# Gated linear attention in one fp32 block kernel: chunk states replaced by direct products, and two output projections in another block order

## The chip, the cores and the metric

One NeuronCore of one Trainium2 chip runs the whole program. The metric is the device time of one execution in microseconds (us), lower is better. The kernel before has a median of 998.92 us over 3 runs (998.89, 998.92, 1001.28).

## The reference

All is float32, 256 tokens, width 1024. Block one is a layer with gated linear attention (GLA) and a layer with sliding-window attention, each with a squared-ReLU MLP; block two has two further attentions, a gated output and an MLP. The change touches the GLA mixer and the code of two projections (`a_w_out` behind the GLA, `w_out_2` in block two). The GLA, cut to what matters:

```python
# 4 heads, key width 128, value width 256, NC = 4 chunks of C = 64 tokens
bcum = jnp.cumsum(heads(gk, GLA_HK), axis=-2)          # log decay inside a chunk
q_t = qf * jnp.exp(bcum);  k_t = kf * jnp.exp(-bcum)
attn = jnp.where(causal, jnp.einsum('nbhik,nbhjk->nbhij', q_t, k_t), 0.0)
o_intra = jnp.einsum('nbhij,nbhjv->nbhiv', attn, vf)
k_dec = kf * jnp.exp(b_last - bcum)
def step(S, xs):
    q_c, k_c, v_c, bl = xs
    o = jnp.einsum('bhik,bhkv->bhiv', q_c, S)
    S = S * jnp.exp(bl)[..., 0, :, None] + jnp.einsum('bhjk,bhjv->bhkv', k_c, v_c)
    return S, o
_, o_inter = lax.scan(step, S0, (q_t, k_dec, vf, b_last))
o = rms(o_intra + o_inter) * g_onorm * silu(gate)
return o @ w_out
```

## The kernel before

The tokens lie in two halves of 128 partitions (c or c2 = 0, 1). Each large weight matrix streams in blocks of 1 MB (2048 columns on 128 partitions). SP loads block j into `raw`; ACT copies it to `whi` as fp32r (`highs_to`), DVE subtracts to get the remainder `wlo` (`lows_to`), and TensorE multiplies activations with both: per k tile two products with `whi` and one with `wlo`. Each of the three buffers has three slots. ACT may fill `whi` for block j once TensorE is through with block j-3; SP may load `raw` for block j once DVE has made the `wlo` of block j-3.

In `gemm_b` a block holds 4 k tiles by 512 columns. TensorE uses it for token half 0 and then for token half 1: 8 products with `whi` and 4 with `wlo`, 512 columns each, for each half. I call these 12 products a block half. A column half f of a 1024-wide result takes two blocks, so four block halves, and all of it is finished before the next column half begins.

The order of work is written out by hand. Each engine has its own program (`tensor_program`, `vector_program`, `scalar_program`, `pool_program`, `sync_program`); Python generators interleave the small attention steps (`attn_gla`, `gates`) between the block halves. Products of the attention run as plain fp32; one such product shows as two records in the trace (a transposition as one). Small products of fp32 write PSUM banks 4 to 7 in turn (`misc`), block results banks 0 to 3 in pairs (`acc_pair`).

The GLA steps on TensorE, between the last blocks of the values `v` and the first of the gates `gt`:

- `kdt`: 8 transpositions of the decayed keys `kd`; ACT copies them out.
- `at`: 8 products of 128 by 128 for the scores inside chunks; DVE copies them under a mask (`copy_predicated`) into `AT`.
- `gs`: 12 products of 256 columns on 64 rows, keys by values, for chunks 0 to 2; DVE copies the first and adds the decayed state before it to the others (`ST`).
- `o`: per token half and pair of heads, 2 products of 256 columns `AT` by `V`, and 64-row-wide results `qt` by `ST` for each chunk but the first; 8 of the first kind and 12 of the second.

ACT copies `o` to `O`, DVE sums squares, POOL makes the factor `o_rstd` by a power, DVE makes the normed and gated `O`. For columns 0 to 511 it folds gate and gain into one factor before the power is there:

```python
t = stt(s, s, st[:, 24 + h * 2 + c:25 + h * 2 + c], g_, ALU.mult, ALU.mult)
if h == 1:
    t.then_inc(*K.up("gated", 0))
```

`turn_parts("to", V.O, half, ...)` on TensorE waits for the event `gated` 0 or 1 and transposes 4 column tiles of `O` (8 transpositions); ACT and DVE split them into `yT`. `gated` 0 is waited for before the last block half of the gates, `gated` 1 inside `project`, behind the first block half of the projection:

```python
g = gemm_b((name,), w, 0, D, xT, lambda k: K.empty((turned, k // 4, (k // 2) % 2)))
next(g)
hook()
```

The blocks of `project` run in the order (k tiles 0-3, columns 0-511), (4-7, 0-511), (0-3, 512-1023), (4-7, 512-1023). DVE adds each finished result to `x`, TensorE transposes the first half of `x` for the next norm before the last block half (`norm_early`).

Of the kernel before, what the change touches and what calls it, by code (L numbers as in the profile page):

```python
# [134 lines left out]
class Views:  # L135


    def __init__(self, S, A):
# [22 lines left out]
        self.kdt = M[:, 7168:8192]  # L161
# [3 lines left out]
        self.ST = M[:, 14336:17408]  # L165
# [68 lines left out]
STEPS = [(p, c) for p in range(2) for c in range(2)]  # L234

# [24 lines left out]
def tensor_program(pe, K, V):  # L260
# [327 lines left out]
    kdt, kt_, qt, VV, AT, ST = V.kdt, V.kt, V.qt, V.V, V.AT, V.ST  # L588
# [52 lines left out]
    def attn_gla():  # L641
        for h2 in range(2):
            tile = ("kdt", h2)
            b = take(tile, misc())
            for w in due(K.at("kd")):
                pe.wait_ge(*w)
            for j in range(2):
                h = 2 * h2 + j
                for c in range(2):
                    t = tr(b[:, j * 256 + c * 128:j * 256 + c * 128 + 128],  # L650
                           V.kd[:, h * 256 + c * 128:h * 256 + c * 128 + 128])
            t.then_inc(*K.filled(tile))
# [12 lines left out]
        v_ready = [K.empty(("v", f, c)) for f in (0, 512) for c in range(2)]  # L665
        def states(h2, *chunks):

            banks_ = [take(("gs", c, h2), misc()) for c in chunks]
            for w in due(K.empty(("kdt", 1)), *v_ready):
                pe.wait_ge(*w)  # L670
            for j in range(2):
                h = 2 * h2 + j
                for c, b in zip(chunks, banks_):
                    rows = slice(64 * (c % 2), 64 * (c % 2) + 64)
                    t = mm(b[:, j * 256:j * 256 + 256],
                           kdt[rows, h * 256 + (c // 2) * 128:h * 256 + (c // 2) * 128 + 128],
                           VV[rows, c // 2, h * 256:h * 256 + 256], True, True)
                    if j == 1:
                        t.then_inc(*K.filled(("gs", c, h2)))

        states(0, 0, 1)
        yield
        states(1, 0, 1)
        yield
        states(0, 2)
        states(1, 2)
        yield
        for c2 in range(2):
            for h2 in range(2):
                tile = ("o", c2, h2)  # L690
                b = take(tile, misc())
                for w in due(K.empty(("at", 1)), K.empty(("gs", 2 * c2, 1))):
                    pe.wait_ge(*w)
                for j in range(2):
                    h = 2 * h2 + j
                    mm(b[:, j * 256:j * 256 + 256], AT[:, h * 256 + c2 * 128:h * 256 + c2 * 128 + 128],
                       VV[:, c2, h * 256:h * 256 + 256], True, False)
                    for c in (2 * c2, 2 * c2 + 1):
                        if c:
                            rows = slice(64 * (c % 2), 64 * (c % 2) + 64)  # L700
                            t = mm(b[rows, j * 256:j * 256 + 256], qt[:, h * 256 + c * 64:h * 256 + c * 64 + 64],
                                   ST[:, (c - 1) * 1024 + h * 256:(c - 1) * 1024 + h * 256 + 256], False, True)
                t.then_inc(*K.filled(tile))
                yield
        yield
        yield
# [7 lines left out]
    def gates_and_scores():  # L714
        yield from gates()
        yield
        for _ in range(4):
# [5 lines left out]
    for _ in range(6):  # L723
        next(gg)
        next(attn, None)
        next(attn, None)
    run_all((attn, 1))
# [380 lines left out]
def vector_program(dve, K, V):  # L1108
# [159 lines left out]
    def project(name, s, hook):  # L1268
        g = gemm_b(D, 8, lambda f, m, c: add_x((name, f, c), f // 512, c))
        next(g)  # L1270
        hook()
        for _ in range(6):
            next(g)
# [81 lines left out]
    bc, e1, qt, kt_, kd, O, ST, AT = V.bc, V.e1, V.qt, V.kt, V.kd, V.O, V.ST, V.AT  # L1355
# [46 lines left out]
    def gates():  # L1402
# [59 lines left out]
    def attn_gla():  # L1462
        for h2 in range(2):
            yield
# [7 lines left out]
            yield  # L1472
        for c in range(3):
            for h2 in range(2):
                tile = ("gs", c, h2)
                for w in due(K.full(tile), *([K.dma("scr1", 1), K.dma("scr2", 2)] if c == 0 else
                                             [K.empty(("gs", c - 1, 0)), K.empty(("gs", c - 1, 1)), K.at("ebl")])):
                    dve.wait_ge(*w)
                for j in range(2):
                    h = 2 * h2 + j  # L1480
                    o = c * 1024 + h * 256
                    b = K.bank(tile)[:, j * 256:j * 256 + 256]
                    if c == 0:
                        t = dve.tensor_copy(ST[:, o:o + 256], b)
                    else:
                        t = stt(ST[:, o:o + 256], ST[:, o - 1024:o - 768], S["ebl"][:, h * 4 + c:h * 4 + c + 1], b,
                                ALU.mult, ALU.add)
                t.then_inc(*K.emptied(tile))
            yield
        for c2 in range(2):  # L1490
            for h2 in range(2):
                for w in due(K.empty(("o", c2, h2))):
                    dve.wait_ge(*w)
                for j in range(2):
                    h = 2 * h2 + j
                    n = h * 2 + c2
                    s = O[:, c2, h * 256:h * 256 + 256]
                    for w in due(*([ev["sq"]] if "sq" in ev else [])):
                        dve.wait_ge(*w)
                    ev["sq"] = step(dve.tensor_tensor_reduce(S["sq"][:, 0:256], s, s, 1.0, 0.0, ALU.mult, ALU.add,  # L1500
                                                             st[:, 8 + n:9 + n]))
                    K.value["o_ssq", 0] = ev["sq"]
                yield
        yield

        for w in due(K.empty(("gt", 0, 0)), K.empty(("gt", 0, 1)), K.dma("bc", 3)):
            dve.wait_ge(*w)
        gain = S["onorm"].rearrange("p (a n) -> p a n", a=1).broadcast_to([128, 2, 256])
        for c in range(2):
            s = V.GT[:, c, 0:512].rearrange("p (a n) -> p a n", a=2)  # L1510
            t = tt(s, s, gain, ALU.mult)
        d = step(t)
        for w in due(K.at("o_rstd"), d):
# [17 lines left out]
    def gates_and_scores():  # L1531
        yield from gates()
        yield
        for _ in range(4):
# [3 lines left out]
    def gated():  # L1538
        for w in due(ev["on"], K.empty(("gt", 512, 0)), K.empty(("gt", 512, 1))):
            dve.wait_ge(*w)  # L1540
        for c in range(2):
            s = O[:, c, 512:1024]
            t = tt(s, s, V.GT[:, c, 512:1024], ALU.mult)
        t.then_inc(*K.up("gated", 1))
# [3 lines left out]
    for _ in range(6):  # L1548
        next(gg)
        next(attn, None)  # L1550
        next(attn, None)
    run_all((attn, 1))
# [4 lines left out]
    gated()  # L1557
# [426 lines left out]
def scalar_program(act, K, V):  # L1984
# [117 lines left out]
    def project(s, hook):  # L2102
        g = gemm_b(D, 8, lambda f, m, c: None)
        next(g)
        hook()
        for _ in range(6):
# [59 lines left out]
    def gates():  # L2166
# [17 lines left out]
        actf(kd, kd, ACT.Exp, scale=-1.0).then_inc(*K.up("g_ekd"))  # L2184
# [20 lines left out]
    def attn_gla():  # L2205
        for h2 in range(2):
            tile = ("kdt", h2)
            for w in due(K.full(tile)):
                act.wait_ge(*w)
            copy(V.kdt[:, h2 * 512:h2 * 512 + 512], K.bank(tile)).then_inc(*K.emptied(tile))  # L2210
            yield
            yield
        for c in range(3):
            yield
        for c2 in range(2):
            for h2 in range(2):
                tile = ("o", c2, h2)
                for w in due(K.full(tile)):
                    act.wait_ge(*w)
                copy(V.O[:, c2, h2 * 512:h2 * 512 + 512], K.bank(tile)).then_inc(*K.emptied(tile))  # L2220
                yield
        yield
        yield
# [7 lines left out]
    def gates_and_scores():  # L2231
        yield from gates()
        yield
        for _ in range(4):
# [5 lines left out]
    for _ in range(6):  # L2240
        next(gg)
        next(attn, None)
        next(attn, None)
    run_all((attn, 1))
# [315 lines left out]
def pool_program(pool, K, V):  # L2560
# [61 lines left out]
    for w in due(K.at("g_eq")):  # L2622
        pool.wait_ge(*w)
    pool.tensor_copy(S["ebl"][:, :], V.qt.rearrange("p (g t) -> p g t", t=64)[:, :, 63:64].rearrange(
        "p g t -> p (g t)")).then_inc(*K.up("ebl"))
    for w in due(K.at("o_ssq")):
# [283 lines left out]
```

## Time and profile before

| what | value |
|---|---|
| median of 3 runs | 998.92 us |
| the profiled execution | 999.79 us |
| its span, first to last instruction | 998.0 us |
| TensorE busy, weight loads busy | 985.3 us (99%), 835.8 us (84%) |
| DVE, ACT, POOL busy | 665.1, 492.0, 36.6 us |
| chain that ended last | TensorE 96%, DVE 2%, ACT 1% |
| mean granted TensorE clock | 0.999 |
| DMA | 177.55 MB, mean 178 GB/s |

The span is what the profile sees of the program; 1.8 us of the execution lie around it. The busy time of TensorE is the union of its products with modelled ends, so it says that the engine is nearly always at work, but not at what rate. The rate is read from the distance between the starts of neighbouring groups in the timeline.

### The profile page before, as it was taken

The page shows a single profiled execution, that of the slowest core. Times are in us where ns is not written, and L with a number is a line of the kernel's source. Part 1 is how long each engine was busy: PE and PEld are TensorE (multiplying, and loading weights), DVE is VectorE, ACT ScalarE, POOL GpSimd, SP SyncE. Part 2 cuts the span into 40 slices and gives each one's busy share as a digit, 9 for nine tenths or more (in the row PEclk, how much of TensorE's full clock was granted, in tenths as well). Part 3 has the DMA queues.
Part 4 walks back from the last instruction along what each step waited for, and adds up shares of the span by engine and source line. Part 5 has one row for each costly group of instructions (what it writes and reads, how often), then busy time and mean ns, then how long its engine had stood idle before and what let it go on. Part 6 is the DMA issues. An engine that isn't in the chain of part 4 may idle for free.

```text
span 998.0 us, 13064 instructions
## 1 busy us (share of the span) xinstructions
PE 985.3 (99%) x5414; PEld 835.8 (84%) x5414; DVE 665.1 (67%) x935; ACT 492.0 (49%) x581; POOL 36.6 (4%) x71
## 2 busy tenths in 40 slices
PE   8999999999999999999999999999999999999997
PEld 8786788888888878888888889888888888888886
DVE  5875766566657976756566658865756675656665
ACT  4453454444446764544444444354554454444454
POOL 2001000000000001000000012000000000000000
PEclk9999999999999999999999999999999999999999
DMA  8652567767653435876675564434165474455551
GB/s 264 191 188 79 178 167 221 214 197 218 212 207 102 127 113 153 245 224 181 191 233 182 199 209 156 157 132 148 56 235 184 148 253 169 169 191 188 190 190 53
DMA packets 113408, 177.55 MB, mean 178 GB/s; under 512 B 4615, under 2 KB 75923, under 8 KB 113348
## 3 DMA queue, kind: packets, MB, share of 16 engines
q1 hardware_dynamic: 113028, 176.37, 55.5%
q8 instruction: 43, 0.70, 0.3%
q10 hardware_dynamic: 320, 0.34, 0.1%
q14 instruction: 17, 0.14, 0.0%
HBM read 174.86 MB, written 1.83 MB: 177 GB/s over the span
## 4 chain that ended last, share of the span: by engine, by line
PE 96%; DVE 2%; ACT 1%; DMA 0%; POOL 0%; issue 0%; ACTq 0%; DVEq 0%; POOLq 0%
PE ps L290 92%; PE ps L294 4%; DVE M L1128 1%; DVE wlo L1120 1%; DMA ident<-in_c_ident 0%; DVE M L1120 0%; POOL st L2573 0%; ACT M L1999 0%; ACT M L1996 0%; DVE cc L1598 0%; DVE RR L1120 0%; POOL st L2570 0%; DVE x L1120 0%; ACT xs L1996 0%; DVE M L1124 0%
## 5 line engine op out<-in xcount | busy, mean ns | idle before, releaser
L290 PE MATMUL ps<-whi,RR 128*128 128x512 f32 (+1 forms) x1556 | 399.7, 389 | 0.0
L1120 DVE TENSOR_TENSOR wlo<-raw,whi 128x1024 fp32r<-128x1024 f32 (+3 forms) x325 | 374.3, 1194 | 20.7 <-ACT whi L1999 20.3
L1999 ACT ACTIVATE whi<-raw 128x2048 fp32r<-128x2048 f32 x161 | 301.2, 1873 | 166.9 <-PE ps L290 148.4
L290 PEld LDWEIGHTS ps<-whi,RR 128*128 128x128 f32 x1556 | 284.0, 188 | 59.4 <-issue 4.5
L290 PE MATMUL ps<-RR,whi 128*128 128x512 f32 (+1 forms) x1264 | 261.1, 351 | 0.0
L290 PEld LDWEIGHTS ps<-RR,whi 128*128 128x128 f32 x1264 | 200.0, 188 | 28.7 <-issue 3.0
L290 PE MATMUL ps<-wlo,RR 128*128 128x512 f32 (+1 forms) x778 | 220.5, 385 | 0.0
L290 PEld LDWEIGHTS ps<-wlo,RR 128*128 128x128 f32 x778 | 144.2, 188 | 29.6
L1120 DVE TENSOR_TENSOR M<-M,ps 128x512 f32<-128x512 f32 (+1 forms) x57 | 38.7, 682 | 172.0 <-ACT M L1999 167.9
L290 PEld LDWEIGHTS ps<-RR,wlo 128*128 128x128 f32 (+1 forms) x1016 | 138.1, 190 | 9.2 <-DVE wlo L1120 0.7
L290 PE MATMUL ps<-RR,wlo 128*128 128x256 f32 (+1 forms) x1016 | 144.5, 282 | 0.0
L1999 ACT ACTIVATE M<-ps 128x512 f32<-128x512 f32 (+2 forms) x90 | 55.2, 615 | 142.8 <-PE ps L290 117.0
L1999 ACT ACTIVATE RR<-M 128x512 fp32r<-128x512 f32 x48 | 30.4, 633 | 71.1 <-DVE M L1128 71.1
L290 PE MATMUL ps<-M 128*64 128x128 f32 (+7 forms) x424 | 55.3, 335 | 0.4 <-DVE M L1120 0.4
L290 PEld LDWEIGHTS ps<-M 128*64 128x64 f32 (+4 forms) x424 | 35.1, 160 | 13.4 <-issue 9.9
L1999 ACT ACTIVATE RR<-ps,G 128x256 fp32r<-128x256 f32 x64 | 25.4, 476 | 32.2 <-PE ps L294 31.8
L2570 POOL TENSOR_SCALAR st<-st 128x2 f32<-128x2 f32 (+2 forms) x11 | 5.1, 460 | 857.2 <-ACT xs L1996 536.6
L1128 DVE SCALAR_TENSOR_TENSOR M<-M 128x512 f32<-128x512 f32 (+1 forms) x49 | 34.4, 703 | 1.7
L1120 DVE TENSOR_TENSOR RR<-M,RR 128x512 fp32r<-128x512 f32 x48 | 32.8, 684 | 0.0
L294 PE MATMUL ps<-ident,M 128*128 128x128 f32 (+1 forms) x196 | 28.0, 276 | 4.1 <-DMA ident<-in_c_ident 1.7
L294 PEld LDWEIGHTS ps<-ident,M 128*128 128x128 f32 (+1 forms) x196 | 22.5, 140 | 11.1 <-issue 6.3
L1128 DVE SCALAR_TENSOR_TENSOR RR<-ps,G,RR 128x256 fp32r<-128x256 f32 x64 | 26.5, 476 | 6.3 <-ACT RR L1999 6.3
(103 smaller groups left out, 379.0 us busy)
## 6 DMA issues: line engine op xcount, KB each, us to landing
raw<-in_w_up SPq DMA_DIRECT2D x32, 1024.0 KB, 6.4
raw<-in_w_down SPq DMA_DIRECT2D x32, 1024.0 KB, 5.6
raw<-in_w_ff SPq DMA_DIRECT2D x32, 1024.0 KB, 5.3
raw<-in_w_in SPq DMA_DIRECT2D x23, 1024.0 KB, 5.1
raw<-in_a_w_in SPq DMA_DIRECT2D x11, 1024.0 KB, 5.5
raw<-in_a_w_out SPq DMA_DIRECT2D x4, 1024.0 KB, 5.1
raw<-in_b_w_q SPq DMA_DIRECT2D x4, 1024.0 KB, 4.9
raw<-in_b_w_out SPq DMA_DIRECT2D x4, 1024.0 KB, 5.1
```

The costliest lines, as they stand in the source:

```text
L290: return pe.matmul(out, lhsT, rhs, start=start, stop=stop, skip_group_check=True)
L294: return pe.transpose(out, in_, ident[0:n, 0:n])
L1120: return dve.tensor_tensor(out, a, b, op)
L1128: return dve.scalar_tensor_tensor(out=out, in0=a, scalar=s, in1=b, op0=op0, op1=op1)
L1999: return act.activation(out, in_, ACT.Copy, **k)
L2570: return pool.tensor_scalar(out, a, s1, s2, op0, op1)
```

## The change

In the GLA the states are gone. Inside a token half, the second chunk's queries meet the first chunk's decayed keys directly (`ac`, 8 products of 64 by 64, copied by ACT into the empty quarter of `AT`). Across the halves, the queries of chunks 2 and 3 meet the keys of chunks 0 and 1 (`ax`, 4 products of 128 by 128, copied by ACT into `AX`); the decays that lie between are multiplied into the keys (`kx`) and queries (`qx`) first. The output then takes 8 products `AT` by `V` and 4 products `AX` by `V`. DVE has new small multiplications for `kx` and `qx` and none for states; POOL copies one part of `qx`; the norm of `O` no longer folds the gate in, and both column halves are gated by a multiplication of their own. The order of `o` is by pair of heads instead of by token half. In `project` (both uses) the blocks run over all columns for k tiles 0-3 first, and the hook comes behind two block halves.

```diff
+HALVES = [(0, 0), (0, 512), (4, 0), (4, 512)]
...
     def project(name, w, s, turned, hook, xT=yT):
-        g = gemm_b((name,), w, 0, D, xT, lambda k: K.empty((turned, k // 4, (k // 2) % 2)))
+        def products():
+            parts = xT if isinstance(xT[0], list) else [k_tiles(part) for part in xT]
+            for k0, f in HALVES:
+                j, hi, lo = block(w[k0 * 128:k0 * 128 + 512, f:f + 512], 4, 512)
+                if k0 == 0:
+                    for c, n in enumerate(acc_pair()):
+                        take((name, f, c), n)
+                for c in range(2):
...
+                    yield
+        g = products()
+        next(g)
         next(g)
         hook()
-        for _ in range(6):
+        for _ in range(5):
             next(g)
         norm_early(s)
         run_all((g, 1))
...
     def attn_gla():
         for h2 in range(2):
-            tile = ("kdt", h2)
...
             tile = ("at", h2)
...
-        states(0, 0, 1)
-        yield
-        states(1, 0, 1)
-        yield
-        states(0, 2)
-        states(1, 2)
+        b = take(("ax",), misc())
+        for w in due(K.at("kx"), K.at("qx_first"), K.at("qx_late")):
+            pe.wait_ge(*w)
+        for h in range(4):
+            t = mm(b[:, h * 128:h * 128 + 128], V.kx[:, h, :, :].rearrange("p c t -> p (c t)"),
+                   V.qx[:, h, :, :].rearrange("p c t -> p (c t)"), True, True)
+        t.then_inc(*K.filled(("ax",)))
+        b = take(("ac",), misc())
+        for h2 in range(2):
+            for c2 in range(2):
+                for j in range(2):
+                    a = (2 * h2 + j) * 256 + c2 * 128
+                    n = (2 * h2 + c2) * 64
+                    t = mm(b[64 * j:64 * j + 64, n:n + 64], V.kd[:, a:a + 64], qt[:, a + 64:a + 128], True, True)
+        t.then_inc(*K.filled(("ac",)))
+        yield
+        for c2, h2 in ((0, 0), (1, 0), (0, 1), (1, 1)):
...
+                t = mm(out, AT[:, h * 256 + c2 * 128:h * 256 + c2 * 128 + 128], VV[:, c2, cols], True, c2 == 0)
+                if c2:
+                    t = mm(out, V.AX[:, h * 128:h * 128 + 128], VV[:, 0, cols], False, True)
...
# vector_program
-        tt(kd, kd, V.kT, ALU.mult).then_inc(*K.up("kd"))
+        d = step(tt(kd4[:, :, 0:3:2, :], kd4[:, :, 0:3:2, :], kT4[:, :, 0:3:2, :], ALU.mult))
+        tt(V.kx[:, :, 1, :], kd4[:, :, 1, :], kT4[:, :, 1, :], ALU.mult)
+        for w in due(d, K.at("qt")):
+            dve.wait_ge(*w)
+        tt(V.kx[:, :, 0, :], kd4[:, :, 0, :], ebl4[:, :, 1:2].broadcast_to([128, 4, 64]), ALU.mult).then_inc(*K.up("kx"))
+        tt(V.qx[:, :, 1, :], qt4[:, :, 3, :], ebl4[:, :, 2:3].broadcast_to([128, 4, 64]), ALU.mult).then_inc(
+            *K.up("qx_late"))
...
-        gain = S["onorm"].rearrange("p (a n) -> p a n", a=1).broadcast_to([128, 2, 256])
-        for c in range(2):
-            s = V.GT[:, c, 0:512].rearrange("p (a n) -> p a n", a=2)
-            t = tt(s, s, gain, ALU.mult)
...
-                g_ = V.GT[:, c, h * 256:h * 256 + 256] if h < 2 else S["onorm"]
-                t = stt(s, s, st[:, 24 + h * 2 + c:25 + h * 2 + c], g_, ALU.mult, ALU.mult)
-            if h == 1:
-                t.then_inc(*K.up("gated", 0))
+                t = stt(s, s, st[:, 24 + h * 2 + c:25 + h * 2 + c], S["onorm"], ALU.mult, ALU.mult)
...
-    run_all((attn, 1))
+    gated(0)
     early()
     turn_parts("to", 0, None)
     next(gg)
     run_all((gg, 1))
-    gated()
+    gated(1)
# scalar_program
+        for w in due(K.full(("ax",))):
+            act.wait_ge(*w)
+        copy(V.AX, K.bank(("ax",))).then_inc(*K.emptied(("ax",)))
+        for j in range(2):
+            t = copy(at5[0:64, :, j, :, 64:128],
+                     K.bank(("ac",))[64 * j:64 * j + 64, 0:256].rearrange("p (a c t) -> p a c t", a=2, c=2))
# pool_program
+    pool.tensor_copy(V.qx[:, :, 0, :], V.qt.rearrange("p (h c t) -> p h c t", h=4, c=4)[:, :, 2, :]).then_inc(
+        *K.up("qx_first"))
```

The order on TensorE from the third block of `v` on. In these rows `ps<-whi,RR` and `ps<-wlo,RR` are the two parts of a block half, `ps<-ident,M` are transpositions, `ps<-M` the attention's own products. Before, up to the first states, and then one of the places where the output is made:

```order
L294 MATMUL ps<-ident,M 128x128 x4
L290 MATMUL ps<-whi,RR 128x512 x8
L290 MATMUL ps<-wlo,RR 128x512 x4
L290 MATMUL ps<-M 128x128 x4
...
L290 MATMUL ps<-M 128x256 x8
...
L290 MATMUL ps<-M 128x256
L290 MATMUL ps<-M 64x256 x2
L290 MATMUL ps<-M 128x256
L290 MATMUL ps<-M 64x256 x2
```

Now:

```order
L293 MATMUL ps<-M 128x128 x8
L293 MATMUL ps<-whi,RR 128x512 x8
L293 MATMUL ps<-wlo,RR 128x512 x4
L293 MATMUL ps<-M 128x128 x4
L293 MATMUL ps<-M 64x64 x8
L293 MATMUL ps<-whi,RR 128x512 x8
L293 MATMUL ps<-wlo,RR 128x512 x4
L293 MATMUL ps<-M 128x256 x6
L293 MATMUL ps<-whi,RR 128x512 x8
L293 MATMUL ps<-wlo,RR 128x512 x4
L293 MATMUL ps<-M 128x256 x6
```

Of the attention four groups are left, with one block half between each two, where seven groups stood; the transpositions and the alternation of 128-row and 64-row results are gone, and six block halves follow before the transpositions of `O`.

The order on DVE, from the gates' first column half (`M<-ps,st,xs`) to the event `gated` 0. Before:

```order
L1128 SCALAR_TENSOR_TENSOR M<-ps,st,xs 128x512
L1500 ISA dg,st<-M 128x256
L1500 ISA st 128x1
L1500 ISA dg,st<-M 128x256
L1500 ISA st 128x1
L1120 TENSOR_TENSOR wlo<-raw,whi 128x1024 x2
L1120 TENSOR_TENSOR M<-M,bcs 128x512 x2
L1128 SCALAR_TENSOR_TENSOR M<-M,st 128x256 x4
L1128 SCALAR_TENSOR_TENSOR M<-M,st,bcs 128x256 x4
```

Now:

```order
L1123 TENSOR_TENSOR wlo<-raw,whi 128x1024 x2
L1131 SCALAR_TENSOR_TENSOR M<-ps,st,xs 128x512 x2
L1131 SCALAR_TENSOR_TENSOR M<-M,st,bcs 128x256 x8
L1123 TENSOR_TENSOR wlo<-raw,whi 128x1024 x2
L1123 TENSOR_TENSOR M<-M 128x512 x2
```

`gated` 0 was raised by the fourth of the multiplications with `st`; it is now raised by the last row shown, behind all eight and behind the remainder of one weight block, which had stood ahead of them.

The order on TensorE inside the projection, from its first block half. Before:

```order
L290 MATMUL ps<-whi,RR 128x512 x8
L290 MATMUL ps<-wlo,RR 128x512 x4
L294 MATMUL ps<-ident,M 128x128 x8
L290 MATMUL ps<-whi,RR 128x512 x8
L290 MATMUL ps<-wlo,RR 128x512 x4
```

Now:

```order
L293 MATMUL ps<-whi,RR 128x512 x8
L293 MATMUL ps<-wlo,RR 128x512 x4
L293 MATMUL ps<-whi,RR 128x512 x8
L293 MATMUL ps<-wlo,RR 128x512 x4
L297 MATMUL ps<-ident,M 128x128 x8
```

The 8 transpositions that wait for `gated` 1 stand one block half later, counted from the projection's first product.

## Rows read from the trace of the kernel before

**Rows 1.** The page, busy time and share, and the granted clock by slice.

```profile
PE 985.3 (99%) x5414; PEld 835.8 (84%) x5414; DVE 665.1 (67%) x935; ACT 492.0 (49%) x581; POOL 36.6 (4%) x71
...
PEclk9999999999999999999999999999999999999999
```

**Rows 2.** What TensorE waited for between 60 and 200 us: total, times, longest.

```profile
PE ps L294 <- DVE M L1120: 1.1, 1, 1.1
```

**Rows 3.** Timeline of TensorE: start us, busy us, line, tile, records.

```profile
57.41 1.98 PE L290 MATMUL ps<-whi,RR 128*128 128x512 f32 x8
...
60.14 0.60 PE L294 MATMUL ps<-ident,M 128*128 128x128 f32 x4
...
63.35 1.05 PE L290 MATMUL ps<-M 128*128 128x128 f32 x8
64.16 2.07 PE L290 MATMUL ps<-whi,RR 128*128 128x512 f32 x8
...
71.15 2.00 PE L290 MATMUL ps<-M 64*128 64x256 f32 x16
...
83.25 4.80 PE L290 MATMUL ps<-M 128*128 128x256 f32 x20
...
90.83 2.39 PE L290 MATMUL ps<-M 128*128 128x256 f32 x12
...
96.02 1.98 PE L290 MATMUL ps<-whi,RR 128*128 128x512 f32 x8
```

**Rows 4.** Timeline of the weight loads inside `o`, 83 to 88 us.

```profile
84.35 0.30 PEld L290 LDWEIGHTS ps<-M 128*128 128x128 f32 x2 [0.39 <-issue]
84.97 0.19 PEld L290 LDWEIGHTS ps<-M 128*64 128x64 f32 x2 [0.33 <-issue]
85.55 0.30 PEld L290 LDWEIGHTS ps<-M 128*128 128x128 f32 x2 [0.39 <-issue]
```

**Rows 5.** Timeline of TensorE in block two's attention, 690 to 718 us.

```profile
690.84 1.53 PE L290 MATMUL ps<-M 128*64 128x128 f32 x24
692.30 1.13 PE L290 MATMUL ps<-M,xs 128*128 128x256 f32 x4
...
716.17 1.03 PE L290 MATMUL ps<-M,xs 128*128 128x256 f32 x4
717.03 1.03 PE L290 MATMUL ps<-M 128*128 128x256 f32 x4
```

**Rows 6.** Timeline of TensorE in the first projection.

```profile
106.94 1.08 PE L290 MATMUL ps<-wlo,RR 128*128 128x512 f32 x4
109.16 1.07 PE L294 MATMUL ps<-ident,M 128*128 128x128 f32 x8 [1.14 <-DVE M L1120]
109.98 2.10 PE L290 MATMUL ps<-whi,RR 128*128 128x512 f32 x8
```

**Rows 7.** Timeline of DVE, 54 to 109 us, pieces.

```profile
54.01 3.48 DVE L1120 TENSOR_TENSOR M<-M 128x1024 f32<-128x1024 f32 x3
...
91.75 0.75 DVE L1128 SCALAR_TENSOR_TENSOR M<-ps,st,xs 128x512 f32<-128x512 f32 x1 [2.12 <-ACT xs L1996]
...
98.63 1.67 DVE L1128 SCALAR_TENSOR_TENSOR M<-M,st 128x256 f32<-128x256 f32 x4 [0.35 <-POOL st L2573]
...
101.81 2.35 DVE L1120 TENSOR_TENSOR wlo<-raw,whi 128x1024 fp32r<-128x1024 f32 x2
...
107.72 1.29 DVE L1120 TENSOR_TENSOR M<-M 128x512 f32<-128x512 f32 x2
```

**Rows 8.** Timeline of ACT around the output of the attention.

```profile
80.50 0.60 ACT L1999 ACTIVATE M<-ps 128x512 f32<-128x512 f32 x1 [10.35 <-PE ps L290]
...
91.03 0.69 ACT L1996 ACTIVATE xs<-ps,st 128x512 f32<-128x512 f32 x1 [2.34 <-PE ps L290]
```

**Rows 9.** Timeline of POOL, the power for the norm of `O`.

```profile
96.07 2.52 POOL L2573 TENSOR_TENSOR st<-st,half_ 128x8 f32<-128x8 f32 x1
```

**Rows 10.** The page, DMA issues: KB each, us from issue to landing.

```profile
raw<-in_a_w_out SPq DMA_DIRECT2D x4, 1024.0 KB, 5.1
```

More of the change, by code:

```diff
@@ L663, in attn_gla @@
             t.then_inc(*K.filled(tile))
-            yield
[L665 to L669, printed above, removed]
+        yield
[14 more added lines that the diff above has]
+        t.then_inc(*K.filled(("ac",)))
+        yield
+        for c2, h2 in ((0, 0), (1, 0), (0, 1), (1, 1)):
+            tile = ("o", c2, h2)
+            b = take(tile, misc())
+            for w in due(K.empty(("at", 1)), K.empty(("ax",)), K.empty(("ac",)),
+                         *[K.empty(("v", 512 * h2, c)) for c in range(2)]):
                 pe.wait_ge(*w)
@@ L672, in states @@
                 h = 2 * h2 + j
[L673 to L679, printed above, removed]
-        states(0, 0, 1)
-        yield
-        states(1, 0, 1)
-        yield
-        states(0, 2)
-        states(1, 2)
[L687 to L703, printed above, removed]
+                out, cols = b[:, j * 256:j * 256 + 256], slice(h * 256, h * 256 + 256)
+                t = mm(out, AT[:, h * 256 + c2 * 128:h * 256 + c2 * 128 + 128], VV[:, c2, cols], True, c2 == 0)
+                if c2:
+                    t = mm(out, V.AX[:, h * 128:h * 128 + 128], VV[:, 0, cols], False, True)
+            t.then_inc(*K.filled(tile))
+            if c2:
                 yield
-        yield
-        yield
     attn = attn_gla()
@@ L716, in gates_and_scores @@
         yield
-        for _ in range(4):
+        for _ in range(3):
             next(attn)
@@ L1268, in project, with products @@
     def project(name, s, hook):
-        g = gemm_b(D, 8, lambda f, m, c: add_x((name, f, c), f // 512, c))
+        def products():
+            for k0, f in HALVES:
+                take()
+                for c in range(2):
+                    if k0:
+                        add_x((name, f, c), f // 512, c)
+                    yield
+        g = products()
+        next(g)
         next(g)
         hook()
-        for _ in range(6):
+        for _ in range(5):
             next(g)
@@ L1490, in attn_gla @@
[L1490 to L1502, printed above, removed]
+        yield
@@ L1533, in gates_and_scores, with gated @@
         yield
-        for _ in range(4):
+        for _ in range(3):
             next(attn)
             yield
-    def gated():
-        for w in due(ev["on"], K.empty(("gt", 512, 0)), K.empty(("gt", 512, 1))):
+    def gated(half):
+        f = 512 * half
+        for w in due(ev["on"], K.empty(("gt", f, 0)), K.empty(("gt", f, 1))):
             dve.wait_ge(*w)
         for c in range(2):
-            s = O[:, c, 512:1024]
-            t = tt(s, s, V.GT[:, c, 512:1024], ALU.mult)
-        t.then_inc(*K.up("gated", 1))
+            s = O[:, c, f:f + 512]
+            t = tt(s, s, V.GT[:, c, f:f + 512], ALU.mult)
+        t.then_inc(*K.up("gated", half))
     run_all((k_and_v(), 1), (gates_and_scores(), 1))
@@ L2102, in project, with products @@
     def project(s, hook):
-        g = gemm_b(D, 8, lambda f, m, c: None)
+        def products():
+            for _ in HALVES:
+                take()
+                for c in range(2):
+                    yield
+        g = products()
+        next(g)
         next(g)
         hook()
-        for _ in range(6):
+        for _ in range(5):
             next(g)
@@ L2205, in attn_gla @@
     def attn_gla():
-        for h2 in range(2):
-            tile = ("kdt", h2)
+        yield
+        for w in due(K.full(("ax",))):
+            act.wait_ge(*w)
+        copy(V.AX, K.bank(("ax",))).then_inc(*K.emptied(("ax",)))
+        at5 = V.AT.rearrange("p (a j c t) -> p a j c t", a=2, j=2, c=2)
+        for w in due(K.full(("ac",)), K.empty(("at", 1))):
+            act.wait_ge(*w)
+        for j in range(2):
+            t = copy(at5[0:64, :, j, :, 64:128],
+                     K.bank(("ac",))[64 * j:64 * j + 64, 0:256].rearrange("p (a c t) -> p a c t", a=2, c=2))
+        t.then_inc(*K.emptied(("ac",)))
+        yield
+        for c2, h2 in ((0, 0), (1, 0), (0, 1), (1, 1)):
+            tile = ("o", c2, h2)
             for w in due(K.full(tile)):
                 act.wait_ge(*w)
[L2210 to L2220, printed above, removed]
+            copy(V.O[:, c2, h2 * 512:h2 * 512 + 512], K.bank(tile)).then_inc(*K.emptied(tile))
+            if c2:
                 yield
-        yield
-        yield
     attn = attn_gla()
@@ L2233, in gates_and_scores @@
         yield
-        for _ in range(4):
+        for _ in range(3):
             next(attn)
```

76 lines of the change are left out of this document (35 added, 41 removed).

## Prediction

> **What bounds the kernel now.** I read the page first: TensorE is busy 99% of the span and the next engine, DVE, 67% [rows 1]; the granted clock reads 9 (full, the 2.4 GHz level) in every slice. The view of waits has one entry between 60 and 200 us, 1.1 us, on DVE [rows 2]. So what counts is time on TensorE, and waits that the change makes or removes there. Busy time has modelled ends, therefore I price work by the distance between starts in the timeline of TensorE.
>
> The unit is the block half of 12 products: from 57.41 to 60.14 there is one, 2.7 us (2.72 over several) [rows 3]. From the first attention transpositions at 60.14 to the block half at 96.02 there are 35.9 us. By the order of the program 7 block halves lie in it, 7 x 2.72 = 19.0 us. **The attention thus costs TensorE 16.8 us now**, any wait inside included. Those are `kdt`, `at`, `gs` and `o`.
>
> **What the attention costs after the change.** Each kind from its nearest row.
> - `at`, 8 products of 128 by 128, unchanged: four take 64.16 - 63.35 = 0.81 us, and the block half behind them shows 2.07 where it shows 1.98 otherwise [rows 3], so 0.1 at the end of each group: 2 x 0.81 + 0.1 = 1.7.
> - `ax`, 4 products of the same form: 0.8.
> - `ac`, 8 products with 64 columns on both sides, alternating between the two column halves of the array. Nearest are 12 products of 128 columns that alternate in the same way, 692.30 - 690.84 = 1.46 us or 0.24 per pair [rows 5]. Four pairs cost 1.0 if fewer columns save nothing, 0.5 if they halve it. A change between full-width and half-width results has a price as well (next point), 0.2 to 0.4 for the way in and out. I take 0.9 with ends 0.5 and 1.4.
> - `o`, 12 products of 256 columns, all full width. There are two prices. Inside the old `o` a full-width product takes 84.97 - 84.35 = 0.62 us and the half-width one behind it 0.58 [rows 4]. In block two's attention, where no half-width product stands between, two take 717.03 - 716.17 = 0.86, so 0.43 each [rows 5]. The new `o` is in the second situation: 12 x 0.43 + 2 x 0.1 = 5.4 us. With 0.62 it would be 7.6.
>
> The sum is 1.7 + 0.8 + 0.9 + 5.4 + 0.1 behind `ac` = 8.9 us, and **the saving 16.8 - 8.9 = 7.9 us**, between 8.5 (all low ends) and 5.2 (the high `ac` and 0.62 per product).
>
> The Trainium skill, TensorEngine Tiling (Array Packing), Overview, "Key Properties", says that changing the tiling mode drains the engine. By it the 0.62 belongs to the alternation and the new `o` costs 5.4, as the two rows have it. The same page's "Instruction Overhead" speaks against the change, at `ac`: it warns against taking the tiling factor from a dimension that is already small, and puts some 60 cycles of overhead on each product. As an estimate from that page, 16 records at 60 cycles of 2.4 GHz are 0.4 us more, so 1.3 for `ac` and a saving of 7.5; no row here has a product this narrow.
>
> **The waits.**
> - *`gated` 1 (in the projection), removed.* The last part of the block half starts at 106.94 and lasts 0.91 to the next start; the transpositions could start at 107.85 and start at 109.16 [rows 6]: 1.3 us, of which the profile shows 1.14 as idle. Behind two block halves instead of one there are 2.7 us more. The saving is 1.3.
> - *`gated` 0 (before the gates' last block half), new.* I count from E, the end of the gates' fourth block half, the one that completes columns 0 to 511. Now it lies at 90.83 [rows 3]. ACT starts the sigmoid at 91.03 [rows 8], DVE the product with it at 91.75 [rows 7]: E + 0.9. That takes 0.7. Then come, by the new order, 8 multiplications (98.63 to 101.81, 3.2 us), the remainder of a weight block (2.35), and the two gating products (107.72, TensorE starts at 109.16, so 1.4 to the release) [rows 6, 7]. Sum: E + 8.6. TensorE has three block halves and is there at E + 8.2. Before, there was a fourth half and part of the attention behind E, and `gated` 0 waited neither for the last four multiplications nor for the remainder. **A new wait of 0.4 us.**
> - *The remainder itself* is ready at E + 7.2, and TensorE wants it for the third of those halves after its 8 products with `whi`, E + 5.4 + 1.8 = 7.2. That is no margin; but what is lost here is not lost again at `gated` 0, since both hang on one chain.
> - *`gated` 1, second look.* The gates' last half ends near E + 12.2; sigmoid, product and gating take 0.9 + 0.7 + 1.4, so E + 15.2. TensorE arrives two block halves after 12.2, at E + 17.6. No wait, 2.4 us spare.
> - *New work on DVE before the scores.* The three multiplications from 54.01 last 3.5 us [rows 7]; the third becomes four smaller ones with 1280 columns instead of 1024, under 1 us more. `ax` stands 4.5 us behind 60.14, so they end long before. POOL's copy of 256 columns is free in the same way: POOL is busy 4% [rows 1].
> - *New copies on ACT.* `AX` is a copy of 512 columns, 0.6 us, like one that ACT now does after 10.35 us idle [rows 8]; the two for `ac` are smaller. Between `ac` and the first `o` lies a block half of 2.7 us. Cost 0; without that half, some 1.5 us.
> - *POOL's power* takes 2.5 us [rows 9]. The squares are done a few us after the last `o`, three block halves before E, so it ends before E. Cost 0.
> - *Fewer operations on DVE* (12 for the states, 2 for the folded gain, against 2 more gating products) shorten nothing by themselves, as DVE isn't the bound.
> - *The order of the blocks in both projections.* The same products and loads, so 0. Columns 0 to 511 are finished at the sixth block half instead of the fourth; their addition to `x` (0.7 us, as other 512-column operations on DVE) is needed by the transpositions behind the seventh, 2.7 us later. In block two's projection TensorE waits for nothing now, and gains nothing.
>
> **Sum.** 7.9 + 1.3 - 0.4 = 8.8 us. The profiled execution took 999.79 us, so its like should take 991.0; the median shown is 0.9 lower, and against it I get 998.92 - 8.8 = **990.1 us**.
>
> **Rivals.**
> 1. *The chain to `gated` 0 is longer than counted.* The saving on TensorE is there, but it arrives earlier at a chain that runs over ACT and DVE, and each us of slip on it is a us of wait. For it: no margin at the remainder, a table load on ACT, ACT and DVE in written order. Against: DVE has less to do before E. One to 3.5 us of slip: 991.1 to 993.6. Chance 0.13.
> 2. *The full-width products keep their 0.62 us.* For it: it is the row of exactly this product [rows 4]. Against: 0.43 in [rows 5]. 12 x 0.19 = 2.3 us more: 992.4. Chance 0.06.
> 3. *The weights come too late* once TensorE uses them faster. A block takes 5.1 us to land [rows 10], TensorE uses one in 5.4 us elsewhere, and SP may issue it only when a remainder three blocks back is made. If this took back 6 us or more, the result would be within 0.3%: 996 to 998. Against: the rest of the kernel lives at that rate without waits [rows 2]. Chance 0.04.
> 4. *Slower: the clock.* If the wait at `gated` 0 grew to several us, TensorE could drop to its 1.2 GHz level and all that follows would cost twice as much until it rises. To be slower than 998.92 + 3, wait and slow work together must take 11.8 us; a wait of 4 us and 7.8 us of work at half rate would do: 1002. Idle of 1.14 us leaves the clock at full [rows 1, 2], so it decides only from a wait well beyond that. Chance 0.03. The Trainium skill, TensorE: Matmul & The Clock Gate, Part 1, has the half rate as the default that activity releases; by it a long enough idle brings this case about, and no row in this stretch shows it.
>
> **How the numbers follow.** The forecast has 0.74. Its own range is 989.0 to 991.5: ends of the product prices but for rival 2 (0.6 each way), the new wait between 0 and 1 us. The low end of the whole range is 988.8, with a little for the scatter of medians. Upwards it takes in rivals 1 and 2: 993.8. A difference of 0.3%, 3 us, is about what a measurement of this kernel can tell from none. Faster by more than that: 0.74 + 0.13 + 0.06 = 0.93; within it 0.04; slower 0.03.
>
> **What would show it.** In the timeline of TensorE after the change: about 8.9 us of attention beside its block halves, from the first `at` to the end of the last `o`; 0.43 us between starts of the new `o` products (rival 2: 0.62); `ac` in about 0.9 us; a wait for DVE under 1 us before the first transpositions of `O`, none before the second; granted clock 9 throughout. The prediction is wrong if TensorE waits over 1 us anywhere between 60 and 130 us, or if the mlp behind the projection waits for weights.

## Result and profile after

| | before | after |
|---|---|---|
| median | 999.45 us (4 runs, 998.89 to 1001.28) | 990.51 us (4 runs, 990.32 to 991.03) |
| ratio | 1 | 0.9906, 95% interval 0.9895 to 0.9918 |
| span of the profiled execution | 998.0 us | 988.5 us |
| from the first attention group to the end | 937.9 us | 928.2 us |
| waits of TensorE shown between 60 and 130 us | 1.1 us | none |

The forecast was 990.1 us, with 989.0 to 991.5 for its own case. The medians differ by 8.9 us and the ratio says 9.4 (8.2 to 10.5). The fourth row of the table is the one that I compare in all runs: the span less the start of the first attention group on TensorE (60.14 before [rows 3], 60.31 after). What TensorE does ahead of that start, the first blocks, the change doesn't touch; the start itself lies between 59.0 and 61.0 us in the profiled runs, and such a difference would hide terms of a few tenths.

The page of the changed kernel, the lines that answer to [rows 1]:

```profile
PE 977.5 (99%) x5390; PEld 834.8 (84%) x5390; DVE 661.0 (67%) x926; ACT 492.1 (50%) x582; POOL 37.9 (4%) x72
...
PEclk9999999999999999999999999999999999999999
```

TensorE has 7.8 us less busy time, and is still at 99%. DVE has lost 4 us and ACT nothing, and neither would have shown that the kernel became 9 us faster.

The timeline of TensorE after the change (start us, busy us, line, tile, records), to be held against [rows 3] and [rows 6]:

```profile
60.31 1.95 PE L293 MATMUL ps<-M 128*128 128x128 f32 x16
62.01 2.07 PE L293 MATMUL ps<-whi,RR 128*128 128x512 f32 x8
63.92 1.07 PE L293 MATMUL ps<-wlo,RR 128*128 128x512 f32 x4
64.83 1.67 PE L293 MATMUL ps<-M 128*128 128x128 f32 x24
66.42 2.12 PE L293 MATMUL ps<-whi,RR 128*128 128x512 f32 x8
68.38 1.08 PE L293 MATMUL ps<-wlo,RR 128*128 128x512 f32 x4
69.30 2.75 PE L293 MATMUL ps<-M 128*128 128x256 f32 x12
71.70 2.20 PE L293 MATMUL ps<-whi,RR 128*128 128x512 f32 x8
...
74.66 2.75 PE L293 MATMUL ps<-M 128*128 128x256 f32 x12
...
80.02 1.98 PE L293 MATMUL ps<-whi,RR 128*128 128x512 f32 x8
...
92.71 1.10 PE L293 MATMUL ps<-wlo,RR 128*128 128x512 f32 x4
93.92 1.06 PE L297 MATMUL ps<-ident,M 128*128 128x128 f32 x8
...
97.57 1.98 PE L293 MATMUL ps<-whi,RR 128*128 128x512 f32 x8
...
102.10 1.07 PE L293 MATMUL ps<-wlo,RR 128*128 128x512 f32 x4
103.02 1.03 PE L297 MATMUL ps<-ident,M 128*128 128x128 f32 x8
```

From 60.31 to the block half at 80.02 there are 19.7 us with 4 block halves in them, 10.9 us; the attention takes 8.8 us. `at` takes 62.01 - 60.31 = 1.70, `ax` and `ac` together 66.42 - 64.83 = 1.59, six `o` products 71.70 - 69.30 = 2.40. These 2.40 us are not six whole products: the first record of the block half starts 0.03 us behind the last record of the group, and the block half then takes 2.96 instead of 2.72. The price is read inside the group, where a stretch near its end begins with this record:

```profile
71.45 0.59 PE L293 MATMUL ps<-M 128*128 128x256 f32 x2
```

It is the eleventh of the twelve, so ten records take 71.45 - 69.30 = 2.15, and a product of two records 0.43 us. The transpositions at 93.92 start 0.3 us later than the block half ahead of them allows (92.71 + 0.91 = 93.62): that is the new wait at `gated` 0. It is too short for the view of waits; it is found from the starts. Those at 103.02 follow without a gap (102.10 + 0.91).

The granted clock with the stages of both kernels, busy time of TensorE in each (stretch, length, busy, records, clock, DMA share, GB/s). Before:

```profile
60.14:105.08 44.94, 44.94 (x217) 1.00 0.33 117
105.08:130.07 24.99, 23.85 (x113) 1.00 0.73 198
130.07:308.31 178.24, 178.24 (x913) 1.00 0.66 203
```

After:

```profile
60.31:97.57 37.26, 37.16 (x193) 1.00 0.44 143
97.57:121.15 23.58, 23.58 (x113) 1.00 0.72 210
121.15:299.39 178.24, 178.24 (x913) 1.00 0.67 202
```

These are the same stages: attention with the gates, the first projection, the first MLP. They give 7.7, 1.4 and 0.0 us. The three parts sum to 9.1 us, and 0.6 us are missing to the 9.7 us between 937.9 and 928.2: they come behind 299 us, far from the GLA and not in the projection of block two either. No step of the prediction has them. The run banks_back below looks for them.

### The profile page after: what moved, and what is told of

Its sections match the earlier page's. It is cut to its first block, busy times and chain, and to the rows that moved or that the text cites. A ratio compares the mean times of both kernels' runs of the same rounds, so it can differ in the third digit from the quotient of the medians.

```text
span 988.5 us, 13010 instructions
## 1 busy us (share of the span) xinstructions
PE 977.5 (99%) x5390; PEld 834.8 (84%) x5390; DVE 661.0 (67%) x926; ACT 492.1 (50%) x582; POOL 37.9 (4%) x72
## 4 chain that ended last, share of the span: by engine, by line
PE 96%; DVE 2%; ACT 1%; DMA 0%; issue 0%; POOL 0%; ACTq 0%; POOLq 0%
PE ps L293 93%; PE ps L297 4%; DVE wlo L1123 1%; DMA ident<-in_c_ident 0%; DVE RR L1131 0%; DVE M L1131 0%; ACT M L1990 0%; DVE M L1123 0%; ACT M L1993 0%; POOL st L2575 0%; DVE cc L1592 0%; ACT RR L1993 0%; ACT xs L1990 0%; DVE x L1131 0%; DVE x L1123 0%
## 5 line engine op out<-in xcount | busy, mean ns | idle before, releaser
L1993 ACT ACTIVATE M<-ps 128x512 f32<-128x512 f32 (+3 forms) x91 | 55.3, 609 | 128.9 <-PE ps L293 105.6
L293 PE MATMUL ps<-M 128*64 128x128 f32 (+7 forms) x408 | 48.7, 322 | 0.5 <-DVE M L1123 0.5
L1990 ACT ACTIVATE M<-M,cc 128x128 f32<-128x128 f32 (+2 forms) x40 | 21.6, 542 | 17.9 <-DVE cc L1744 9.9
```

Of the source, the lines that this page charges most:

```text
L293: return pe.matmul(out, lhsT, rhs, start=start, stop=stop, skip_group_check=True)
L1990: return act.activation(out, in_, f, **k)
L1993: return act.activation(out, in_, ACT.Copy, **k)
```

## Experiments

All times in the column are the span less the start of the first attention group, from one profiled execution each; the ratio is of the timed runs to those of the kernel before beside them.

| run | start to end, us | against | ratio, 95% interval |
|---|---|---|---|
| before | 937.9 | | |
| after | 928.2 | -9.7 | 0.9906 (0.9895 to 0.9918) |
| gla_only | 929.0 | +0.8 to after | 0.9914 (0.9901 to 0.9928) |
| order_only | 936.5 | -1.4 to before | 0.9983 (0.9974 to 0.9993) |
| gate_early | 927.9 | -0.3 to after | 0.9904 (0.9891 to 0.9918) |
| hook_late_old_order | 930.9 | +2.7 to after | 0.9937 (0.9923 to 0.9950) |
| grouped | 936.4 | -1.5 to before | 0.9985 (0.9975 to 0.9994) |
| ax_ac_mixed | 929.2 | +1.0 to after | a single run |
| ac_twice | 928.7 | +0.5 to after | a single run |
| banks_back | 928.8 | +0.6 to after | a single run |
| gate_later | 929.3 | +1.1 to after | 0.9912 (0.9897 to 0.9927) |
| after_again | 928.2 | 0.0 to after | 0.9898 (0.9884 to 0.9913) |
| gate_early_again | 927.9 | -0.3 to after | 0.9896 (0.9880 to 0.9913) |

The intervals are 0.2 to 0.3% wide, 2 to 3 us. For most of these terms the timed runs only say that nothing large is missing; the terms themselves are read in the timeline.

### The two parts alone

The new GLA with the old `project`:

```diff
+        g = gemm_b((name,), w, 0, D, xT, lambda k: K.empty((turned, k // 4, (k // 2) % 2)))
         next(g)
         hook()
-        for _ in range(5):
+        for _ in range(6):
```

> The new GLA with the old projection code. Theory (TensorE's time is the sum of its work and its waits): gating for gated 1 starts on DVE at 99.57 in the changed kernel and releases 1.4 us later, 101.0; with the old order TensorE gets there at 97.57 + 2.72 = 100.3, so a wait of 0.7 us. Span 988.5 + 0.7 = 989.2 us. Rival (the new projection order gives the whole 1.3 us that it was credited with): span 989.8. Rival (the order does nothing once the GLA is short, since DVE has less to do): 988.5.

TensorE in this run, inside the projection:

```profile
96.52 1.98 PE L293 MATMUL ps<-whi,RR 128*128 128x512 f32 x8
98.33 1.07 PE L293 MATMUL ps<-wlo,RR 128*128 128x512 f32 x4
99.95 1.06 PE L297 MATMUL ps<-ident,M 128*128 128x128 f32 x8 [0.56 <-DVE M L1101]
```

98.33 + 0.91 is 99.24, the transpositions start at 99.95: a wait of 0.7 us, as expected. The span of this run is 988.2 us, which taken by itself would say that nothing was lost; but its first attention group starts at 59.24 instead of 60.31. From there to the end it is 0.8 us longer than the changed kernel. So beside the new GLA, the new order is worth 0.7 to 0.8 us and not the 1.3 us that it was credited with: with the new GLA the chain on DVE is already ahead. The sigmoid of the last gates waits on ACT for a product on DVE; it starts 1.0 us behind the end of the gates in the kernel before (106.11 against 105.08) and 0.4 us behind it here (96.94 against 96.52). The sum of the prediction is right nevertheless, because it counts a wait as removed, by whichever part.

The old GLA with the new `project`:

```diff
+        def products():
+            for k0, f in HALVES:
```

> The old GLA with the new projection code. Theory: TensorE gets to the transpositions for gated 1 one block half later, at 110.6 where the release is at 109.2, so the wait of 1.3 us goes and nothing else changes: span 998.0 - 1.3 = 996.7 us, no wait behind it up to the mlp. Rival (the later finish of columns 0 to 511 moves a wait to norm_early or to the mlp): span 997.3 or more, with a wait of DVE or ACT before the x transpositions.

```profile
109.82 1.08 PE L292 MATMUL ps<-wlo,RR 128*128 128x512 f32 x4
110.73 1.04 PE L296 MATMUL ps<-ident,M 128*128 128x128 f32 x8
111.53 2.09 PE L292 MATMUL ps<-whi,RR 128*128 128x512 f32 x8
```

The wait of [rows 6] is gone and none stands in its place: 1.4 us less from the attention to the end (1.3 expected), span 996.8 us.

Whether it is the order of blocks or the place of the hook was told apart by the old order with the hook behind two block halves:

```diff
         g = gemm_b((name,), w, 0, D, xT, lambda k: K.empty((turned, k // 4, (k // 2) % 2)))
         next(g)
+        next(g)
         hook()
-        for _ in range(6):
+        for _ in range(5):
```

> The changed kernel with the old order of blocks in the projections, the hook still behind two block halves. Theory: the second block now needs k tiles 4-7 at once; the first remainder of the split is on DVE at 104.28 + 0.7 = 105.0 where TensorE is ready at 103.8, so a wait of 1.1 to 1.2 us, and one like it in block two's projection: span 988.5 + 2.3 = 990.8 us. Rival (the place of the hook alone brings the gain, the order of blocks none): 988.5.

```profile
102.95 1.03 PE L297 MATMUL ps<-ident,M 128*128 128x128 f32 x8
105.06 2.09 PE L293 MATMUL ps<-whi,RR 128*128 128x512 f32 x8 [1.07 <-DVE RR L1102]
...
757.77 1.03 PE L297 MATMUL ps<-ident,M 128*128 128x128 f32 x8
759.87 2.08 PE L293 MATMUL ps<-whi,RR 128*128 128x512 f32 x8 [1.07 <-DVE RR L1102]
```

In both projections the block half behind the transpositions starts 2.1 us after them instead of 0.8: 1.3 us each, 2.7 in all (2.3 expected; in each the block half starts 0.1 to 0.2 us later than I had counted). TensorE waits for the split of the tiles that it has just transposed. The late hook needs the new order, since only then do two block halves that don't need them come next.

### The chain to `gated` 0

In the first of these runs DVE norms and gates columns 0 to 511 before the weight remainder and the other columns:

```diff
-        for h in range(4):
-            for c in range(2):
...
-        ev["on"] = step(t)
-        yield
+        for half in range(2):
+            for h in (2 * half, 2 * half + 1):
+                for c in range(2):
...
+            ev["on"] = step(t)
+            if half == 0:
+                gated(0)
+            yield
...
-    gated(0)
     early()
```

> The changed kernel, where DVE norms and gates columns 0 to 511 first (4 multiplications and 2 gating products), then makes the weight remainder, then norms the other columns. Theory: the wait of 0.3 us at gated 0 goes, since its release falls from E + 8.5 to about E + 4.7, and the remainder is ready at E + 6.7 for a need at E + 7.2: span 988.5 - 0.3 = 988.2 us. Rival (the wait is on something else, the transpositions' bank or the sigmoid on ACT): it stays, 988.5.

TensorE and DVE in this run:

```profile
93.42 1.07 PE L293 MATMUL ps<-wlo,RR 128*128 128x512 f32 x4
94.33 1.03 PE L297 MATMUL ps<-ident,M 128*128 128x128 f32 x8
```

```profile
87.76 1.67 DVE L1131 SCALAR_TENSOR_TENSOR M<-M,st,bcs 128x256 f32<-128x256 f32 x4
89.46 1.29 DVE L1123 TENSOR_TENSOR M<-M 128x512 f32<-128x512 f32 x2
90.67 2.35 DVE L1123 TENSOR_TENSOR wlo<-raw,whi 128x1024 fp32r<-128x1024 f32 x2
92.94 1.67 DVE L1131 SCALAR_TENSOR_TENSOR M<-M,st,bcs 128x256 f32<-128x256 f32 x4
```

The gating ends near 90.7 and TensorE comes at 94.33, without a gap (93.42 + 0.91). The time from the attention to the end is 0.3 us less.

In the second run one multiplication more stands ahead of the gating:

```diff
+    tt(e1, e1, bc, ALU.mult)
     gated(0)
     early()
```

> The changed kernel with one more multiplication of 1024 columns on DVE (1.2 us, into a buffer that is not read any more) right before the two gating products of gated 0. Theory (one chain sets the release, and TensorE waits for its end, us for us): the wait before the first transpositions of O grows from 0.3 to 1.5 us, and the time from the first attention products to the end from 928.2 to 929.4 us; the clock stays at its full level. Rival (other work takes the slip up): under 0.6 us more. Rival (the clock falls with the longer wait): over 3 us more.

```profile
93.19 1.12 PE L293 MATMUL ps<-wlo,RR 128*128 128x512 f32 x4
95.54 1.06 PE L297 MATMUL ps<-ident,M 128*128 128x128 f32 x8 [1.23 <-DVE M L1123]
```

The third block half starts at 91.38 and ends at 94.10; the wait is 1.4 us, and the whole is 1.1 us longer. So the chain is one, and rival 1 of the prediction had the right price: the wait grows by 1.1 us for the 1.14 us that DVE is longer at work. The granted clock between 60 and 130 us is 1.00 in this run; an idle of 1.23 us doesn't lower it. Waits of several us, on which rival 4 rested, were not tried.

To see whether gate_early is better in time as well, it ran once more beside the changed kernel:

> The changed kernel as it is, on the chip of the run beside it, to compare with gate_early_again: ratio to before 0.991.

> The changed kernel with columns 0 to 511 normed and gated first, once more, beside the changed kernel itself. Theory: no wait before the first transpositions of O, 0.3 us less than the changed kernel from the first attention products to the end (927.9 against 928.2); in the whole time 0.3 us less, which is less than the scatter of the runs. Rival: no difference in the profile.

The profile repeats itself: 928.2 and 927.9 us, and TensorE's transpositions follow the block half without the gap. The medians are 989.86 and 990.17 us, with runs from 989.13 to 991.57: the 0.3 us can't be told in the time. The profile shows a wait less, and the timed runs show no difference between the two.

### What a product costs beside another width

The kernel before, with each output tile's full-width products first and the half-width ones behind them:

```diff
                     mm(b[:, j * 256:j * 256 + 256], AT[:, h * 256 + c2 * 128:h * 256 + c2 * 128 + 128],
                        VV[:, c2, h * 256:h * 256 + 256], True, False)
+                for j in range(2):
+                    h = 2 * h2 + j
                     for c in (2 * c2, 2 * c2 + 1):
```

This order changes the sums: the second start in a bank comes before the first sum in it is complete, and the outputs are not those of the reference. The number of products and their shapes are the same, so it serves for the time alone. The Trainium skill, PSUM — Partial Sum Buffer, "The four PSUM rules", has a product with the start flag clear the accumulation bits of a whole zero region; by that part of the first sum would be lost, and no run here examined it.

> The kernel before, where each output tile takes its two full-width products first and its half-width ones behind them, so that each of the four tiles changes width 2 times instead of 4. Theory (a change between full-width and half-width results costs 0.19 us each, which is where 0.62 against 0.43 came from): 8 changes less, 1.5 us less; from the first attention transpositions to the end 937.9 - 1.5 = 936.4 us. Rival (0.62 and 0.58 are the price of these products, whatever stands beside them): 937.9.

TensorE, the group that answers to the x20 in [rows 3] and the one behind it:

```profile
82.98 4.11 PE L290 MATMUL ps<-M 128*128 128x256 f32 x20
87.02 2.12 PE L290 MATMUL ps<-whi,RR 128*128 128x512 f32 x8
...
89.89 2.04 PE L290 MATMUL ps<-M 128*128 128x256 f32 x12
91.86 2.11 PE L290 MATMUL ps<-whi,RR 128*128 128x512 f32 x8
```

The x20 group takes 4.04 us instead of 4.73, the x12 group 1.97 instead of 2.32, the tile ahead of them 0.34 us less as well. That is 1.4 us for 8 changes of width, 0.17 each (0.19 expected), and 1.4 to 1.5 us in the whole, the spans being rounded to 0.1. The products are the same in number and shape, so 0.62 was not the price of the product. It closes the sum too: of the 0.62 + 0.58 us in [rows 4] two changes are 0.34, and 0.86 are left for two products, 0.43 for the full-width and 0.43 for the half-width one.

The reverse in the changed kernel, each `ax` product followed by two of `ac`:

```diff
         for h in range(4):
             t = mm(b[:, h * 128:h * 128 + 128], V.kx[:, h, :, :].rearrange("p c t -> p (c t)"),
                    V.qx[:, h, :, :].rearrange("p c t -> p (c t)"), True, True)
+            h2, c2 = h // 2, h % 2
+            for j in range(2):
```

> The changed kernel, where each ax product is followed by two ac products, so 8 changes of width instead of 2 in that group. Theory as in the run before: 6 x 0.19 = 1.1 us more in that group, which takes 1.59 us now: 2.7. Rival (the price lies in the products): 1.6.

```profile
64.75 2.70 PE L293 MATMUL ps<-M 128*128 128x128 f32 x24
67.37 2.11 PE L293 MATMUL ps<-whi,RR 128*128 128x512 f32 x8
```

2.62 us instead of 1.59 for the same 12 products: 1.03 us for 6 changes more, 0.17 each again. The same figure comes from the other side and in another kernel, there with 128 and 64 columns instead of 256: what costs is the change of width, not the product. The 0.17 us are the mean of a way in and a way out. The Trainium skill, TensorEngine Tiling (Array Packing), Overview, "Key Properties", says that a change of mode drains the engine; the traces agree that a change costs time, 0.17 us here; what the engine does in it they don't show.

What is left of the group was measured by doubling `ac`:

```diff
-        for h2 in range(2):
+        for h2 in (0, 1, 0, 1):
```

> The changed kernel with the 8 ac products issued twice over the same outputs. Theory (the group takes 1.59 us, 0.81 of it ax, 0.38 two changes of width, so 0.4 is left for 8 products): 0.4 us more, 2.0 for the group. Rival (a narrow product costs as much as one of 128 columns, 0.24 per pair, and a change of width nothing): 1.0 us more, 2.6.

```profile
63.56 2.13 PE L293 MATMUL ps<-M 128*128 128x128 f32 x40
65.62 2.12 PE L293 MATMUL ps<-whi,RR 128*128 128x512 f32 x8
```

2.06 us against 1.59: 8 narrow products cost 0.47 us, 0.12 per pair. The 0.24 per pair with 128 columns that the prediction took from [rows 5] is too high for a comparison, since those 1.46 us hold a part of the changes of width at both ends. Inside that group of the kernel before, two stretches begin with these records:

```profile
691.22 1.15 PE L290 MATMUL ps<-M 128*64 128x128 f32 x18
...
691.87 0.50 PE L290 MATMUL ps<-M 128*64 128x128 f32 x6
```

Twelve records, three pairs, lie between them: 0.65 us, 0.22 per pair. So half the columns cost a little more than half the time, and what doesn't go with the columns is at most 0.02 us per pair. With two changes of width `ac` is 0.47 + 2 x 0.17 = 0.8 us, and with `ax` 0.8 the group is complete. The estimate of 1.3 us that I made from the same page's "Instruction Overhead", by adding 60 cycles for each record, is too high here. The same passage also has a matmul with a free dimension of 1 take as long as one with 60; by that 64 columns lie just above the limit, and no product here is narrow enough to show it.

### The half microsecond behind 300 us

The GLA used 14 small PSUM tiles before and 8 now, and these take banks 4 to 7 in turn. So each later tile that takes its bank in this turn has another one, two further; some tiles have banks of their own, the query product among them. The profile before has a wait of 0.69 us on ACT at 318.90, ahead of `ps<-dg,ones`, which spreads the norm's factor; after the change there is none. The run turns the banks back:

```diff
+    turn["misc"] += 2
     next(gg)
```

> The changed kernel with the turn of PSUM banks 4 to 7 moved on by two behind the GLA, so that all later small products get the banks that they had before the change. Theory: the product that spreads the norm's factor over the rows, at 309.4 now, takes bank 6 again and waits for ACT's copy of the query product out of it; the wait of 0.7 us on ACT that the kernel before shows at 318.9 comes back, and about 0.5 us in all. Rival (that wait moved with ACT's timing): no wait on ACT there, nothing added.

TensorE there, before:

```profile
317.57 0.64 PE L290 MATMUL ps<-RR,wlo 128*128 128x256 f32 x4
318.90 0.70 PE L290 MATMUL ps<-dg,ones 128*128 128x256 f32 x2 [0.69 <-ACT M L1999]
```

After:

```profile
308.65 0.64 PE L293 MATMUL ps<-RR,wlo 128*128 128x256 f32 x4
309.39 0.70 PE L293 MATMUL ps<-dg,ones 128*128 128x256 f32 x2
```

In banks_back:

```profile
308.87 0.64 PE L293 MATMUL ps<-RR,wlo 128*128 128x256 f32 x4
310.20 0.70 PE L293 MATMUL ps<-dg,ones 128*128 128x256 f32 x2 [0.69 <-ACT M L1994]
```

The wait is back with the same 0.69 us, and the time from the attention to the end rises by 0.6 us, which is all that was missing. In the kernel before this product takes bank 6, out of which ACT must first copy the query product; after the change it takes bank 4, and the query product is in bank 6 as before. The 0.6 us are a by-product of the number of small tiles that the GLA uses.

## Why the prediction was right, and where it was off

- *What bounds the kernel.* Right: every us that TensorE was given or spared is found again in the time from the attention to the end, in all eleven runs.
- *The attention costs 16.8 us now and 8.9 us after.* 8.8 us measured. By kind, expected and measured with the tail behind each group: `at` 1.7 and 1.7 (1.8 with the tail), `ax` 0.8, `ac` 0.9 and 0.1 behind them against 1.59 for both (1.75 with the tail), `o` 5.4 against 2 x (2.40 + 0.24) = 5.3.
- *The choice between 0.62 and 0.43 us per `o` product*, the step with most in it (2.3 us). It was made by what stands beside the product in the row, and is right: 0.43 us inside the group. The two runs on the width show why. Rival 2 falls.
- *`gated` 1, 1.3 us.* The first projection's stage is 1.4 us shorter. The share of the new order in it is 0.7 to 0.8 us beside the new GLA.
- *The new wait of 0.4 us at `gated` 0.* 0.3 us measured. Counted from E, here 85.46, the release was expected at 8.6 and TensorE started at 93.92, E + 8.5. The weight remainder was in time within a few hundredths: the `wlo` part at 92.71 lasts 1.10 instead of 1.07. Rival 1 had the right mechanism, and no slip.
- *Costs set to nothing.* The copies on ACT, POOL's copy and power, the multiplications on DVE and the later sums in `x` added no wait. Rival 3, late weights, falls for the stretch up to the first MLP: that takes 178.24 us in both kernels.
- *What the sum missed.* 0.6 us behind 300 us. No step of the prediction has the turn of the PSUM banks: where it takes the removed tiles out of the attention, it counts the products and copies that go with them, and not that tiles behind them then land in other banks. It adds to the 0.1 us from the attention, 0.1 from the projection and 0.1 from the smaller wait, so that the profile gained 9.7 us where I had 8.8.
- *Luck in the time.* That the median came within 0.4 us of the forecast is in part chance. The forecast starts from a median of 998.92 us before; with the fourth run it is 999.45, 0.5 higher, and this about makes up for the 0.6 us that no step has. The single terms are borne out by the timeline, not by this agreement.
- *Rival 4, the clock.* Not met; the clock is at its 2.4 GHz level in each stretch, with idle up to 1.23 us in gate_later.

## What to carry to other kernels

On an engine that is busy all the time, price work by the distance between starts in the timeline, and take the price from a row in which the neighbours are of the kind that the new code will have: here the neighbours made 0.2 us of 0.6. When a change removes tiles from a pool that is dealt out in turn, look at what bank each later tile gets, since the order of instructions won't show it. And compare profiled runs from a common event on, not by their spans, when the terms are smaller than the scatter of the start.

## What the runs showed of the hardware that I had not expected

A change between full-width and half-width results costs 0.17 us on TensorE, the same in two kernels and in both directions of the test (8 changes less, 1.38 us less; 6 more, 1.03 us more). Half-width fp32 products of 64 columns cost 0.12 us per pair, those with 128 columns 0.22, so hardly any cost per product that doesn't go with the columns shows down to that size.
